# Five wide projection groups computed as three products of high and low parts, with the index choice placed by hand

## The reference

```
h = RMSNorm(x)
h @ w_in -> [qa 512 | ka 128 | va 128 | qi 512 | ki 64 | wi 8 | qb 512 | kb 512 | vb 512 | gate_a 1024 | gate_b 1024]
rotary on the first 16 of the 64 dims of every q and k
branch A: I[t,s] = sum_h w[t,h] * relu(q_idx[t,h] . k_idx[s]); each prompt query attends to the 128 keys
          with the largest I; k_a, v_a, k_idx are outputs as well
branch B: block-sparse attention with qb, kb, vb; k_b, v_b are outputs as well
x += (sigmoid(gate_a) * (o_a @ w_br_a) + sigmoid(gate_b) * (o_b @ w_br_b)) @ w_out
x += expert layer (top-1 group, top-2 of its 8 experts), then a last RMSNorm
```

## Time and profile before

| | |
|---|---|
| time, median of three runs | 1133.3 us (1132.47 to 1134.33) |
| span of the profiled execution, first to last instruction | 1126.7 us |
| time of the profiled execution as a whole | the page gives its span only; 1133.3 - 1126.7 = 6.6 us lie around it by the median |
| PE busy, PEld, DVE, ACT, POOL | 943.2, 550.1, 411.5, 274.3, 161.2 us |
| wide groups of `project` on PE | 39.18 to 208.0 us |
| first instruction of `prompt` on PE | 211.12 us |

### The profile page before, as it was taken

How to read it: one execution, slowest core, us unless ns; L and a number is a source line. 1 busy time by engine, 2 the same in 40 slices (tenths; PEclk the granted TensorE clock), 3 DMA queues, 4 the chain that set the end, 5 groups by cost and what they waited for, 6 DMA issues and landing times. The chain is left out here.

```text
span 1126.7 us, 14438 instructions
## 1 busy us (share of the span) xinstructions
PE 943.2 (84%) x5797; PEld 550.1 (49%) x5797; DVE 411.5 (37%) x899; ACT 274.3 (24%) x496; POOL 161.2 (14%) x200
## 2 busy tenths in 40 slices
PE   6999999888789999649969999999759996677760
PEld 4544444455556666234557999845623332222220
DVE  3213698566539595110206332112341110111116
ACT  4112221355536777302110000001200110000002
POOL 1200000222012235312330000000011111100010
PEclk9999999899999999869998999999769999998985
DMA  8221120123347987977965842086369999999966
GB/s 273 95 75 58 45 87 20 48 68 95 113 170 269 355 329 247 389 278 276 372 248 130 244 154 57 1 291 241 125 213 369 375 364 369 361 373 360 370 216 238
DMA packets 139265, 246.83 MB, mean 219 GB/s; under 512 B 12432, under 2 KB 104704, under 8 KB 130880
## 3 DMA queue, kind: packets, MB, share of 16 engines
q1 hardware_dynamic: 116944, 142.64, 37.9%
q0 software_dynamic: 21488, 101.05, 24.5%
q10 hardware_dynamic: 768, 2.23, 0.5%
HBM read 238.50 MB, written 15.77 MB: 226 GB/s over the span
## 5 line engine op out<-in xcount | busy, mean ns | idle before, releaser
L692 PE MATMUL bank<-ring,hT 128*128 128x512 f32 (+1 forms) x384 | 161.8, 576 | 0.0
L692 PEld LDWEIGHTS bank<-ring,hT 128*128 128x128 f32 x384 | 72.5, 193 | 79.7 <-issue 71.0
L2128 PE MATMUL bank<-early,obT 128*64 128x512 f32 x352 | 87.2, 646 | 22.7 <-DMA early<-in_w_e_up 21.2
L1353 ACT COPY kT_s<-bank 128x1024 f32<-128x1024 f32 (+1 forms) x90 | 85.5, 996 | 43.4 <-PE bank L1111 43.3
L1111 PEld LDWEIGHTS bank<-consts,ring 128*128 128x128 f32 x704 | 76.1, 141 | 39.3 <-ACT kT_s L1353 35.1
L1111 PE MATMUL bank<-consts,ring 128*128 128x128 f32 x704 | 87.6, 277 | 2.9 <-PEq L236 2.0
L2334 DVE TENSOR_TENSOR uT<-uT,bank 128x256 f32<-128x256 f32 x16 | 6.7, 421 | 206.4 <-ACT uT L2183 206.4
L2128 PEld LDWEIGHTS bank<-early,obT 128*64 128x64 f32 x352 | 28.5, 148 | 79.5 <-issue 56.4
L1783 PE MATMUL bank<-w_o,uT 128*128 128x512 f32 x128 | 55.6, 593 | 2.6 <-PEq L250 2.6
L1604 PE MATMUL bank<-hT_hi,gate_w_hi 128*128 128x272 f32 x192 | 56.5, 294 | 0.0
L1604 PE MATMUL bank<-hT_hi,gate_w_lo 128*128 128x272 f32 x192 | 55.4, 289 | 0.0
(11 more groups left out here) (372 smaller groups left out, 1463.4 us busy)
## 6 DMA issues: line engine op xcount, KB each, us to landing
early<-in_w_e_gate SPq DMA_DIRECT2D x44, 512.0 KB, 7.9
early<-in_w_e_up SPq DMA_DIRECT2D x44, 512.0 KB, 8.8
early<-in_w_e_down SPq DMA_DIRECT2D x12, 1024.0 KB, 11.0
ring<-in_w_in SPq DMA_DIRECT2D x5, 2048.0 KB, 8.3
early_gates<-in_w_e_down SPq DMA_DIRECT2D x10, 1024.0 KB, 11.2
w_o<-in_w_e_gate SPq DMA_DIRECT2D x20, 512.0 KB, 8.9
w_o<-in_w_e_up SPq DMA_DIRECT2D x20, 512.0 KB, 9.9
uT<-in_w_e_down SPq DMA_DIRECT2D x10, 1024.0 KB, 11.0
```

The costliest lines, as they stand in the source:

```text
L692: last = nc.tensor.matmul(bank[:, n % 4, 0:WID[g]], s.hT[:, k, t * P:(t + 1) * P], w[:, gi % 2, k, 0:WID[g]], start=(k == 0), stop=(k == K ...
L1353: nc.scalar.copy(kT[:, n % 2, u, :], bank[:, u, :]).then_inc(kT_kept, 1)
L2128: last = nc.tensor.matmul(bank[half(u), 2, :], xT[:, slot % 2, k, half(u)], gate_up_at(s, slot)[:, u, k, :], start=(k == 0), stop=(k == KD ...
```

## The change

The `kv` group stays as it was, tile by tile with plain products. For the five wide groups:

- The prompt tiles' products become three `F32R` products each (`split_products`). The parts of `hT` are made once per tile (high on ScalarE, `round_hT`; low on VectorE, `rest_hT`), before the first wide group starts. The parts of the weights are made per slice of 128 x 512 (40 in all): high on ScalarE (`round_chunk`), low on GpSimd. There is one buffer each for `w_hi` and `w_lo`; a slice is overwritten with the next group's once tiles 1 to 3 have used it (`chunk_used`), the last one once the whole group is done.
- The order inside a wide group is: tile 0 through all eight slices; the sample tile, plain as before; then slice by slice tiles 1, 2 and 3 together. Transposes of tiles 1 to 3 are carried into the next group; index scores sit at named places (`INDEX_AT`), the rounds of the choice as well.
- Weights arrive as halves of 1 MB in a ring of three (`raw`); a half is freed by the sample item.
- The stores of `kv` and `kb` move from GpSimd's queue to SyncE's, between the weight loads; the work on the page table moves from the end of the block into the first wide group.
- `project` no longer lies in `s.ring`: the ring, `oaT`, `obT` and `branch_w` are given out after it, and `project` and `prompt` get a cleanup of semaphores each instead of one together.

The diff, cut to its core:

```diff
-            s.oaT = sa("oaT", [P, PAIRS, NTOK])
-            s.obT = sa("obT", [P, PAIRS, NTOK])
-            s.bw = sa("branch_w", [P, 2, 2, PAIRS, P])
...
-                s.ring = ss("ring", [P, NR, SLOT_B * QW])
...
+                    with nc.cleanup_on_exit():
+                        project(nc, s, a, o)
+
+                    s.oaT = sa("oaT", [P, PAIRS, NTOK])
+                    s.obT = sa("obT", [P, PAIRS, NTOK])
+                    s.bw = sa("branch_w", [P, 2, 2, PAIRS, P])
+                    s.ring = samp.enter_context(nc.sbuf_tensor("ring", [P, NR, SLOT_B * QW], F32))
+                    with nc.cleanup_on_exit():
+                        prompt(nc, s, a)
                 with nc.cleanup_on_exit():
...
+    FIRST, REST = list(range(TT)), [0, TP, 1, 2, 3]
+    ITEMS = [(g, t) for gi, g in enumerate(GROUPS) for t in (REST if gi else FIRST)]
...
+    NRAW = 3
...
-    IDX0 = 2 * TT
+
+    INDEX_AT = {(2, k): k - 1 for k in range(1, KD)} | {(3, "first"): 7, (3, "sample"): 8} | {(3, k): 9 + k for k in range(3)}
     ROUNDS = [(t, r) for t in (3, 2, 1) for r in range(TOPK_P // 8)]
-    ROUND0 = IDX0 + 1 + PAIRS
...
+        raw = sb("w_raw", [P, NRAW, KD // 2, 512])
+        w_hi, w_lo = sb("w_hi", [P, KD, 512]), sb("w_lo", [P, KD, 512])
+        hTh, hTl = sb("hT_hi_p", [P, KD, SEQ]), sb("hT_lo_p", [P, KD, SEQ])
...
+        def item(gi, t):
+            return TT * gi + (REST if gi else FIRST).index(t)
+
+        def carried(gi):
+
+            if gi == 0 or GROUPS[gi - 1] == "vb":
+                return []
+            return [TT * gi - 1] if gi == 1 else [TT * gi - 3, TT * gi - 2, TT * gi - 1]
...
+            def load_half(gi, q):
+                m = 2 * (gi - 1) + q
+                if m >= NRAW:
+                    sp.wait_ge(raw_used, (m - NRAW) // 2 + 1)
+                c, n = COLS[GROUPS[gi]][0]
+                sp.dma_start(raw[:, m % NRAW, :, :], w_in[:, q * KD // 2:(q + 1) * KD // 2, c:c + n]).then_inc(raw_in[m], 16)
...
-            weights(0)
+            load_kv()
...
+            load_half(1, 0)
+            load_half(1, 1)
...
-            for gi in range(2, len(GROUPS)):
-                sp.wait_ge(w_used, gi - 1)
-                weights(gi)
+            load_half(2, 0)
+            for n in range(TT):
+                store(n)
+            load_half(2, 1)
+            load_half(3, 0)
+            load_half(3, 1)
+            load_half(4, 0)
+            store(item(3, 0))
+            load_half(4, 1)
+            load_half(5, 0)
+            store(item(3, TP))
+            for t in range(1, TP):
+                store(item(3, t))
+            load_half(5, 1)
...
+            for i in range(NNAT):
+                sp.wait_ge(stored[i], nat_stores(len(natural), i))
             sp.wait_ge(vb_stored, 16 * TT)
-
...
-            for n, (g, t) in enumerate(ITEMS):
-                if g not in ("kv", "kb"):
-                    continue
-                pool.wait_ge(rot_ready, order[n] + 1)
...
+            for gi in range(1, NG_IN):
+                for k in range(KD):
+                    pool.wait_ge(hi_ready, KD * (gi - 1) + k + 1)
+                    nc.gpsimd.tensor_tensor(w_lo[:, k, :].bitcast(F32R), raw_w(gi, k), w_hi[:, k, :], ALU.subtract)\
+                        .then_inc(lo_ready, 1)
...
+            def round_hT(t):
+                act.wait_ge(hT_kept, 2 * t + 2)
+                cols = slice(t * P, (t + 1) * P)
+                nc.scalar.copy(hTh[:, :, cols].bitcast(F32R), s.hT[:, :, cols]).then_inc(hTh_ready, 1)
+
+            def round_chunk(gi, k):
+
+                if k % (KD // 2) == 0:
+                    act.wait_ge(raw_in[half_of(gi, k)], 16)
+                if gi >= 2 and k < KD - 1:
+                    act.wait_ge(chunk_used, (KD - 1) * (gi - 2) + k + 1)
+                if gi >= 2 and k == KD - 1:
+                    act.wait_ge(proj_done, TT * gi)
+                nc.scalar.copy(w_hi[:, k, :].bitcast(F32R), raw_w(gi, k)).then_inc(hi_ready, 1)
...
-            for n in range(len(ITEMS)):
+            for n in range(TT):
                 if n + 2 < TT:
                     square(n + 2)
                     root(n + 2)
                 if n + 1 < TT:
                     keep_hT(n + 1)
...
+                    round_hT(n - 1)
+                if n == TP - 1:
+                    for k in range(KD // 2):
+                        round_chunk(1, k)
+            for k in range(KD // 2, KD):
+                round_chunk(1, k)
+            for gi in range(1, NG_IN):
+                carry = carried(gi)
+                turns = GROUPS[gi] != "vb"
+                keep_projected(item(gi, 0))
+                for m in carry[0:1]:
+                    keep_transposed(m)
+                index_relu(gi, "first")
+                keep_projected(item(gi, TP))
+                for m in carry[1:2]:
+                    keep_transposed(m)
+                index_relu(gi, "sample")
+                for k in range(KD):
+                    if gi + 1 < NG_IN:
+                        round_chunk(gi + 1, k)
+                    if k == 0:
...
+                for t in range(1, TP):
+                    keep_projected(item(gi, t))
...
+            def rest_hT(t):
+                cols = slice(t * P, (t + 1) * P)
+                dve.wait_ge(hTh_ready, t + 1)
+                nc.vector.tensor_tensor(hTl[:, :, cols].bitcast(F32R), s.hT[:, :, cols], hTh[:, :, cols], ALU.subtract)\
+                    .then_inc(hTl_ready, 1)
...
-                if n in order:
-                    dve.wait_ge(nat_ready, n + 1)
-                    b = nat[:, order[n] % NNAT, :]
-                    if t < TP:
-                        prompt_rows(g, t, b)
-                    else:
-                        sample_rows(g, b)
-                if 0 <= n - IDX0 - 1 < len(IDX):
-                    index_sum(n - IDX0 - 1)
-                if n >= ROUND0:
-                    items = len(ITEMS) - ROUND0
...
-            dve.wait_ge(table_in, 16)
...
+                rotated(n)
+                if n >= 1:
+                    rest_hT(n - 1)
+            rotated(item(1, 0))
+            page_rows()
+            rotated(item(1, TP))
+            for t in range(1, TP):
+                rotated(item(1, t))
+
+            rotated(item(2, 0))
+            for q in range(1):
+                index_sum(q)
+            rotated(item(2, TP))
+            for q in range(1, PAIRS):
+                index_sum(q)
+            for q in range(PAIRS, 7):
+                index_rounds(q - PAIRS, q - PAIRS + 1)
+                index_sum(q)
+            for t in range(1, TP):
+                rotated(item(2, t))
+            index_sum(7)
+            rotated(item(3, 0))
+            index_sum(8)
+            index_rounds(3, 4)
+            index_sum(9)
+            rotated(item(3, TP))
+            index_sum(10)
+            index_sum(11)
+            index_rounds(4, 12)
+            for t in range(1, TP):
+                rotated(item(3, t))
+            index_rounds(12, 13)
+            rotated(item(4, 0))
+            index_rounds(13, 14)
+            rotated(item(4, TP))
+            index_rounds(14, 26)
+            for t in range(1, TP):
+                rotated(item(4, t))
+            index_rounds(26, len(ROUNDS))
...
-                if t < TP:
-                    for k in range(KD):
-                        last = nc.tensor.matmul(bank[:, n % 4, 0:WID[g]], s.hT[:, k, t * P:(t + 1) * P],
-                                                w[:, gi % 2, k, 0:WID[g]], start=(k == 0), stop=(k == KD - 1))
-                    last.then_inc(proj_done, 1)
-                    return
...
+                if gi >= 1:
+                    pe.wait_ge(proj_done, n + 1)
+                    pe.sem_inc(raw_used, 1)
+
+            def split_products(n, k):
+
+                t = ITEMS[n][1]
+                cols = slice(t * P, (t + 1) * P)
+                x_hi, x_lo = hTh[:, k, cols].bitcast(F32R), hTl[:, k, cols].bitcast(F32R)
+                hi, lo = w_hi[:, k, :].bitcast(F32R), w_lo[:, k, :].bitcast(F32R)
+                for c, (l, m) in enumerate(((x_hi, hi), (x_lo, hi), (x_hi, lo))):
+                    last = nc.tensor.matmul(bank[:, n % 4, :], l, m, start=(k == 0 and c == 0),
+                                            stop=(k == KD - 1 and c == 2))
+                return last
...
-            for n in range(len(ITEMS)):
+            for n in range(TT):
                 if n + 1 < TT:
                     turn_tokens(n + 1)
-                products(n)
-                if n >= 1 and n - 1 in order:
+                if n == 0:
...
+                    plain_products(n)
+                else:
+                    sample_products(n)
+                if n >= 1:
...
-            if len(ITEMS) - 1 in order:
-                transposes(len(ITEMS) - 1)
+            pe.wait_ge(hTl_ready, TP)
+            for gi in range(1, NG_IN):
+                carry = carried(gi)
+                turns = GROUPS[gi] != "vb"
```

(58 more changed lines are left out.)

194 lines of the change are left out of this document (99 added, 95 removed).

## The result

| | before | after |
|---|---|---|
| median, runs side by side on one chip (7 each) | 1132.5 us (1123.5 to 1134.3) | 1120.2 us (1117.8 to 1122.0) |
| ratio of the times, 95% interval | | 0.990 (0.987 to 0.993) |
| span of the profiled execution | 1126.7 us | 1117.6 us |
| first product of the wide groups on TensorE | 39.18 us | 51.02 us |
| `prompt` starts on TensorE | 211.12 us | 198.78 us |

The change gains 12.3 us by the medians, half of the 24 forecast; the forecast was 1109 us with a range of 1102 to 1120. In the profiles `prompt` starts 12.3 us earlier, and what follows takes 3.2 us longer, so the spans differ by 9.1 us only.

What follows compares the result with a forecast made beforehand. TensorE's 320 plain products were taken to bound the stage: products -34.3 us, later start +4.8, clock +2.3; with VectorE ending last, prompt came 24.9 us earlier, less about 1 for edges: -24, from 1133.3 to 1109 us, range 1102 to 1120.

Steps and rivals of the forecast that it cites:

- The start of the first wide group: TensorE waits for the low parts of all four tiles and starts near 44.0 us, 4.8 us later.
- rival C: VectorE becomes the bound by collisions with GpSimd's subtractions, some 6 us, partly at the end; 1112 to 1118 us, chance 0.19.
- The products: On TensorE, 480 F32R records at 0.216 us replace 320 plain ones at 0.431: 103.7 instead of 138.0 us, -34.3.
- Rival B: F32R records miss half of plain's price (0.227 us or more), TensorE's end is the bound; 1112 to 1117 us, chance 0.15.
- the loss of clock: TensorE's clock drops after the gap before the first wide group, costing 2.3 us (0 to 2.5).
- The weights' parts: ScalarE's slices and GpSimd's 40 subtractions, taken at 1.0 us each, are hidden and cost nothing.
- Queues: Weight halves and stores in SyncE's queue come in time and cost nothing; without that slack, a few us once.
- The end of the block: VectorE has the last word or nearly, ending at 185.2 us; stores end at 183.8, prompt begins at 186.2.
- What lies behind the barrier: From prompt's start to the end stays 915.6 us; a change of over 2 us proves the forecast wrong.
- From span to time: Expected span 1103 us plus 6.6 us around it, unchanged, gives 1109 us against the median of 1133.3.

Runs made afterwards that it cites:

- e2: Changed kernel with the first wide group's eight weight subtractions on VectorE instead of GpSimd; median 1110.1 us, ratio to before 0.984.
- e7: e4 with three more rounds of the choice placed earlier in VectorE's row; median 1109.8 us, ratio to before 0.981.
- e8: e4 with 14 extra F32R products behind TensorE's last one, into a bank nobody reads; median 1109.5 us, ratio to before 0.981.
- e9: e4, e7 and e8 together; median 1107.8 us, ratio to before 0.980.
- e3: Changed kernel's order, ring and slices, but with plain products and no low parts; median 1130.8 us, ratio to before 1.000.
- e1: Changed kernel with the parts of hT for tile 3 made ahead of the sample item's rotation; median 1112.2 us, ratio to before 0.985.
- e4: Changed kernel with e1 and e2 together, four subtractions before the sample item's rotation and four behind; median 1110.2 us, ratio to before 0.982.
- e5: Changed kernel with the three products reordered so the two using hT's high part are neighbours; one run, 1125.2 us.

## Why the prediction was wrong

It named `prompt` at 186.2 us and it came at 198.8, 12.6 us later. Three steps make that up: the first wide product came 7.0 us later than forecast (51.0, not 44.0), the groups took 6.4 us longer (143.2, not 103.7 + 30.8 + 2.3 = 136.8), and VectorE's lag behind them was 0.8 us shorter.

**The start of the first wide group: the step that failed.** It counted the operations ahead of `rest_hT(3)` at the durations they had in the kernel before, beside a GpSimd that was idle there (7.2 us of 168.8). It did not lay GpSimd's first eight subtractions beside them, although both are released by the same rounding of the slices. The mechanism stood in the text as rival C, at the wrong place and at half its size: I spread the collisions over the 100 us of VectorE's work in the groups and looked for their cost at the block's end. There they cost little: the 16 first steps of a rotation take 332 ns against 292, 0.6 us in all, and the rounds cost what they did. They fell together where VectorE's row was the critical one and GpSimd had eight operations in a row. e2 shows it: without GpSimd beside it the row of eleven takes 1.8 us instead of 9.0, and the start is 43.79 where I had 44.0. (The two agree better than the steps do: `hT`'s low part was ready at 43.05, and in e2 a low part of a weight stands behind it.)
The Trainium skill (SBUF — State Buffer, "Who interferes with whom") has the rule that the loser waits for the whole instruction, and it names copies and `tensor_scalar` among those that can be caught. The trace comes near it, some 1.0 us of wait at a subtraction of 1.35; the COPY of 1.17 us and the TENSOR_SCALAR of 1.14 agree. I had quoted only its sentence on two inputs.

**The products: 0.216 taken, 0.227 measured.** Rival B, by its lower figure: the 0.011 us over the columns alone are there at 272 columns and at 512, a fixed extra per record. My reading, a weight load that 272 columns do not quite cover and 512 do, was a guess, and it chose the end of the range that suited it. 480 x 0.011 = 5.2 us of the 6.4. The rest: the 23 F32R products that follow another kind of work take 0.31 to 0.34 us to the next start and not 0.227, some 2.1 us in all, which I had not counted; and the loss of clock was 1.4 us in the groups (seven starts at 0.43) and not 2.3.

**The weights' parts: right in the end, off in size.** A subtraction takes 1.3 us, not 1.0; between groups TensorE waits for none (0.2 us in all), as said. ScalarE's 40 slices at 0.62 us are hidden.

**Queues: right.** One copy of ScalarE waited 4.6 us for a store, and nobody behind it.

**The end of the block: right in kind.** VectorE has the last word, 3.1 us behind TensorE (forecast 4.4), with the stores close under it, 0.5 us as e7 shows.

**What lies behind the barrier: 3.2 us off, cause open.** I had said that a change of over 2 us there would prove me wrong. `prompt` has the same instructions and takes 107.0 us instead of 101.7, at a granted clock of 0.89 instead of 0.95. Over the eleven profiles the two go together: 99.9 us at 0.98, 101.4 at 0.97, 102.5 at 0.94, 104.1 at 0.93, 105.4 at 0.91, 107.0 at 0.89, 107.3 at 0.88. In the kernel before TensorE had been idle for 3.2 us when `prompt` began, now for 4.4; with 1.3 and 1.0 us in e8 and e9 the block takes 101.4 and 99.9. But the pause does not set the length: six kernels with 4.4 to 4.6 us of it have 102.5 (e2), 102.5 (e3), 104.1 (e1), 105.4 (e4), 107.0 (after) and 107.2 (e5). What the pause costs for certain is at the first eight records, 0.9 us more than before (3.78 against 2.89). What makes the rest of the 5.3 us is not shown; each kernel has one profile, and that of before was a quick run.

**From span to time.** I added 6.6 us around the span, the difference of a profiled span and a median of other runs. The profiled runs of the kernel after and of the experiments have 1.8 to 2.2 us around theirs (1119.4 against 1117.6): the profile of before was then a quick run, of some 1129 us. It cancels in the difference, but a span may not be set against a median.

So B held, with 5.2 us, and C's collision came at another place, with 7.0. I had priced the two as separate rivals and gave no case to both together; the range ended where the measured time lies.

## What to carry to other kernels

When work moves to an idle engine, lay it beside what VectorE does in the same microseconds and ask which of its rows is critical there: a GpSimd operation of 1.3 us makes every 0.16 us operation beside it last 1.2, and a short row of eleven grows by 7 us. Put what others wait for ahead of the many small operations, or give the first, urgent batch to VectorE itself, so that no GpSimd operation runs beside the row. By the medians the first took 8 us off this kernel, the second 10, and both together 10, with a dozen lines. Where two durations of one operation at two sizes are not to be had, take the extra over the ideal as fixed and not as gone.

## What the runs showed of the hardware

- An F32R product of 128 x 128 by 512 columns starts every 0.227 us at full clock, 0.43 at half; at 272 columns every 0.126. The columns' own share by the plain ones is 0.216 and 0.115: the same 0.011 us more at both widths, in any order of the operands.
- VectorE's COPY of 32 x 128 takes 0.21 us alone and 1.17 beside GpSimd's subtractions; its `max` and `match_replace` over 384 columns, 561 and 542 ns in the mean of 16, are what they were the earlier trace rows.
- A GpSimd copy of 512 columns (0.82 us) holds VectorE's short operations as well, for 0.13 to 0.36 us.
- Behind a pause of 3.9 to 4.6 us the first eight records of `prompt` take 3.59 to 3.79 us (eight kernels), behind 3.2 us 2.89, behind 1.0 and 1.3 us 1.99, full clock. A short pause does not always keep the clock: behind 1.5 us the first eight wide products of e9 start 0.43 us apart, half clock, and those of e4 0.23. What tells the two apart was not found.
